# Feature units in pairs, three broadcasts later, the queries' low halves earlier

## The reference

```python
x = x + sliding_window_attention(rms_norm(x), positions, w_qkv, ..., w_o)
x = x + (silu(h @ w_gate) * (h @ w_up)) @ w_down
x = x + hybrid_mixer(rms_norm_2(x, g_mix), ...)
x = x + memory_cross_attention(rms_norm_2(x, g_cross), rms_norm_2(mem, g_mem), ...)
x = x + conv_glu_ffn(rms_norm_2(x, g_ffn), ...)
return rms_norm_2(x, g_final)
```

## Time and profile before

| | |
|---|---|
| median of three runs | 2711.31 us |
| the profiled execution, its own time | 2711.65 us |
| its span, first to last instruction | 2710.3 us |
| TensorE matmuls busy | 2698.5 us, 100% of the span |
| TensorE weight loads (beside the matmuls) | 2295.3 us, 85% |
| VectorE busy | 1690.4 us, 62% |
| ScalarE busy | 1370.2 us, 51% |
| mean granted clock of TensorE | 0.999 |
| DMA | 183 GB/s mean |

### The profile page before, as it was taken

How to read it: one execution, slowest core, us unless ns; L and a number is a source line. 1 busy time by engine, 2 the same in 40 slices (tenths; PEclk the granted TensorE clock), 3 DMA queues, 4 the chain that set the end, 5 groups by cost and what they waited for, 6 DMA issues and landing times.

```text
span 2710.3 us, 34758 instructions
## 1 busy us (share of the span) xinstructions
PE 2698.5 (100%) x13968; PEld 2295.3 (85%) x13968; DVE 1690.4 (62%) x2420; ACT 1370.2 (51%) x2036; POOL 0.2 (0%) x4
## 2 busy tenths in 40 slices
PE   9999999999999999999999999999999999999999
PEld 8778888888888888888888888888888888888887
DVE  7885666556656664664555655544568756785676
ACT  7875544344434454455444644444455535553554
POOL 0000000000000000000000000000000000000000
PEclk9999999999999999999999999999999999999999
DMA  7335566666665577768686555544556565656554
GB/s 245 125 110 178 186 188 190 194 185 188 194 193 185 189 198 169 172 144 193 185 196 220 174 184 189 189 145 156 185 176 210 182 206 178 197 181 205 186 187 155
DMA packets 257154, 495.64 MB, mean 183 GB/s; under 512 B 17313, under 2 KB 19105, under 8 KB 256482
## 3 DMA queue, kind: packets, MB, share of 16 engines
q1 hardware_dynamic: 256994, 493.43, 59.8%
HBM read 491.27 MB, written 2.10 MB: 182 GB/s over the span
## 4 chain that ended last, share of the span: by engine, by line
PE 98%; ACT 1%; DVE 1%; issue 0%; DMA 0%; SPq 0%; ACTq 0%
PE ps L500 29%; PE ps L489 16%; PE ps L490 16%; PE ps L491 16%; PE ps L505 15%; PE ps L457 2%; PE ps L697 1%; PE ps L613 1%; PE ps L758 1%; PE ps L739 1%; PE ps L590 0%; PE ps L663 0%; PE ps L586 0%; PE ps L650 0%; PE ps L711 0%
## 5 line engine op out<-in xcount | busy, mean ns | idle before, releaser
L954 ACT CAST whi<-raw 128x1024 fp32r<-128x1024 f32 x919 | 966.1, 1052 | 1224.9 <-PE ps L491 627.7
L1395 DVE TENSOR_TENSOR wlo<-raw,whi 128x1024 fp32r<-128x1024 f32 x919 | 1120.3, 1222 | 660.2 <-ACT whi L954 658.7
L500 PE MATMUL ps<-XA,whi 128*128 128x512 f32 x1792 | 449.1, 392 | 0.0
L500 PE MATMUL ps<-XC,whi 128*128 128x512 f32 x1664 | 416.9, 392 | 0.0
L489 PE MATMUL ps<-whi,XB 128*128 128x512 f32 x944 | 370.8, 393 | 2.2 <-issue 2.2
L500 PEld LDWEIGHTS ps<-XA,whi 128*128 128x128 f32 x1792 | 322.6, 189 | 57.9
L491 PE MATMUL ps<-whi,XB 128*128 128x512 f32 x944 | 368.3, 390 | 0.0
L490 PE MATMUL ps<-wlo,XB 128*128 128x512 f32 x944 | 368.2, 390 | 0.0
L500 PEld LDWEIGHTS ps<-XC,whi 128*128 128x128 f32 x1664 | 299.5, 189 | 53.7
L489 PE MATMUL ps<-whi,XA 128*128 128x512 f32 x736 | 292.1, 397 | 1.5 <-DVE wlo L1395 0.9
L491 PE MATMUL ps<-whi,XA 128*128 128x512 f32 x736 | 287.0, 390 | 0.0
(11 more groups left out here) (250 smaller groups left out, 1930.7 us busy)
## 6 DMA issues: line engine op xcount, KB each, us to landing
raw<-in_w_up SPq DMA_DIRECT2D x176, 512.0 KB, 3.6
raw<-in_w_in SPq DMA_DIRECT2D x128, 512.0 KB, 5.1
raw<-in_ffn_w_gate SPq DMA_DIRECT2D x88, 512.0 KB, 3.6
raw<-in_ffn_w_up SPq DMA_DIRECT2D x88, 512.0 KB, 4.1
raw<-in_ffn_w_down SPq DMA_DIRECT2D x88, 512.0 KB, 4.2
raw<-in_w_down SPq DMA_DIRECT2D x88, 512.0 KB, 3.7
raw<-in_w_ckv SPq DMA_DIRECT2D x64, 512.0 KB, 4.3
raw<-in_attn_w_qkv SPq DMA_DIRECT2D x39, 512.0 KB, 3.8
```

The costliest lines, as they stand in the source:

```text
L500: pe.matmul(ps[:, b, :], whi[:, i, j, c], both, start=w.begin and j == 0, stop=False)
L954: act.copy(whi[:, u % NSPL, :, :], raw[:, u % NRAW, :, :]).then_inc(s.hi, 1)
L1395: dve.tensor_tensor(wlo[:, u % NSPL, :, :], raw[:, u % NRAW, :, :], whi[:, u % NSPL, :, :].bitcast(F), ALU.subtract).then_inc(s.lo, 1)
```

## The change

`feature_unit` is cut into `feature_high` (the 8 matmuls with `whi`) and `feature_low` (the 8 with `wlo`). Where a feature unit has an even number, TensorE does its high part alone. At the next unit it does that unit's high part, then the low part of the first, then its own. The high part waits for `hi`, the low part for `lo`. What raises `unit` stays the last matmul of a unit's low part. Work that stands between the two units of a pair (transposes at units 73, 529 and 657) keeps its place ahead of the second unit.

Broadcasts 1, 4 and 5 move from two to four units behind their root, on TensorE and on ScalarE. In VectorE's program `queries_low` moves from the end of the query work to just behind the weight subtraction of its iteration, ahead of the residual sum, the feeds, the chances and `query_scale`.

```diff
--- before.py
+++ after.py
@@ -491,13 +491,18 @@
                     end = pe.matmul(o, xl, whi[:, i, j, :], start=False, stop=w.end and j == 1)
             end.then_inc(s.unit, 1)
 
-        def feature_unit(u, w):
+        def feature_high(u, w):
+
             i = u % NSPL
             for j in range(2):
                 both = X[w.x][:, w.xk + j, :, :]
                 for f in range(4):
                     b, c = w.banks[f], slice(f * P, (f + 1) * P)
                     pe.matmul(ps[:, b, :], whi[:, i, j, c], both, start=w.begin and j == 0, stop=False)
+
+        def feature_low(u, w):
+
+            i = u % NSPL
             for j in range(2):
                 high = X[w.x][:, w.xk + j, 0, :]
                 for f in range(4):
@@ -881,8 +886,10 @@
                     pe.wait_ge(s.ox, 8)
 
         q_turn, p_turn, p_values = later(Q, 4), later(ATTEND, 2), later(ATTEND, 3)
-        wide_at, level_at = later(ROOT, 2), later(LEVEL, 1)
+        wide_at, level_at = {u + (4 if n in (1, 4, 5) else 2): n for u, n in ROOT.items()}, later(LEVEL, 1)
         gla_turn_at, merge_at, c_turn_at = later(GLA, 3), later(MERGE, 25), later(CSC, 2)
+
+        PAIRS = {u for u in range(0, U_END, 2) if UNITS[u].kind == "feature"}
         pe.wait_ge(s.ones, 1)
         warm(8)
         for u, w in enumerate(UNITS):
@@ -929,11 +936,23 @@
                 banks_clear(u, w)
             if u > LAST - 4:
                 continue
-            pe.wait_ge(s.lo if u else s.lo0, u + 1)
             if w.kind == "rows":
+                pe.wait_ge(s.lo if u else s.lo0, u + 1)
                 rows_unit(u, w)
+            elif u - 1 in PAIRS:
+
+                pe.wait_ge(s.hi, u + 1)
+                feature_high(u, w)
+                pe.wait_ge(s.lo, u)
+                feature_low(u - 1, UNITS[u - 1])
+                pe.wait_ge(s.lo, u + 1)
+                feature_low(u, w)
             else:
-                feature_unit(u, w)
+                pe.wait_ge(s.hi, u + 1)
+                feature_high(u, w)
+                if u not in PAIRS:
+                    pe.wait_ge(s.lo, u + 1)
+                    feature_low(u, w)
 
         for u in range(LAST - 3, LAST + 1):
             pe.wait_ge(s.lo, u + 1)
@@ -1255,7 +1274,7 @@
 
         q_root_at, q_turn = later(Q, 2), later(Q, 4)
         p_turn, p_values = later(ATTEND, 2), later(ATTEND, 3)
-        wide_at, gla_root_at, gla_turn_at = later(ROOT, 2), later(GLA, 1), later(GLA, 3)
+        wide_at, gla_root_at, gla_turn_at = {u + (4 if n in (1, 4, 5) else 2): n for u, n in ROOT.items()}, later(GLA, 1), later(GLA, 3)
         merge_at, c_turn_at, level_exp_at = later(MERGE, 25), later(CSC, 2), later(LEVEL, 0)
         tiles1, tiles2 = later(TILES, 1), later(TILES, 2)
 
@@ -1904,6 +1923,8 @@
                 done += 1
             if u in (1, 3, 5):
                 feed(*FEED[u][0], (1,))
+            if u in q_scale:
+                queries_low(q_scale[u])
             if u in RESID and u < U_END:
                 residual(u, RESID[u])
             for n, c, bank in FEED.get(u, []):
@@ -1942,7 +1963,6 @@
                 keys_low()
             if u in q_scale:
                 query_scale(q_scale[u])
-                queries_low(q_scale[u])
             if u in TILES:
                 e, ch, which, f = TILES[u]
                 tile_sum(u, e, ch, which, f)
```

## The result

The changed kernel takes 2703.93 us, the median of 10 runs (2703.78 to 2704.76), against 2711.34 us for the kernel before (10 runs, 2710.18 to 2711.82). The ratio is 0.9974 with a 95% interval of 0.9966 to 0.9982: 7.4 us or 0.27% faster. The forecast was 2703.0. The profiled execution took 2703.85 us, its span is 2702.5 against 2710.3. The executions of the kernel before fall into two groups some 1.5 us apart, those of the changed kernel don't; what that does to the 7.4 us is taken up behind e8.

The account below looks back on a forecast made before the run. TensorE, busy over the whole span, was taken as the bound. The profiled 2711.65 - 4.6 (pairs) - 3.8 (queries' low halves) = 2703.2 us; as that execution lay 0.3 us over the median, 2703.0 was given, range 2700.8 to 2708.4.

Parts of the forecast that it names:

- edit 1: Feature units on TensorE run by twos, 16 highs then 16 lows: 0.022 us saved a pair, -4.6 us in all.
- Edit 3: Queries' low halves made earlier on VectorE, ending TensorE's "issue" wait in unit 45 and the low clock behind: -3.8 us.
- The first step: Unit 45: TensorE starts at 176.09 instead of 178.32, 2.23 us saved.
- The second: Nine matmuls behind unit 45's wait run at full clock, 2.12 instead of 3.70 us: 1.58 us saved.
- the surplus from the grouped rows: Feature units: a train of 8 highs behind lows takes 1.843 us against 1.814, a surplus of 0.029 us.
- Edit 2: Three broadcasts two units later, as pairs delay their identities: cost nothing; without the move about 0.7 us each.
- Buffers: Second feed-forward: the tightest subtraction's slack of 3.45 us shrinks by 1.8 us; 1.6 us left, cost nothing.
- the arrears' three late copies: Second feed-forward "up" chunks: three odd iterations might each add 1.8 us to VectorE's backlog, 5.5 us together.
- Rival C: Second feed-forward: VectorE's backlog makes TensorE wait 2.05 us in each of 11 "up" chunks, about 2726 us; chance 0.05.
- A: Feature units: the surplus grows with the lows, so pairing saves nothing; 2707.5 us, up to 2709; chance 0.23.
- B: Unit 45 is held by something else, or the clock falls anyway: 2706.7 down to 2704.5 us; chance 0.07.
- D: Feature units: no surplus at all after 16 lows, saving 10.8 and 3.8 us: 2696.7 us; chance 0.04.

Follow-up runs that it names:

- e8: Changed kernel with the queries' low halves moved between the chances and the query scale: 2705.51 us.
- e1: Kernel before with only the queries' low halves moved ahead of the chances, feature units singly: 2707.97 us.
- e2: Changed kernel with the queries' low halves back at their old place, pairs and later broadcasts kept: 2707.47 us.
- e7: e1 with low matmuls of 320 instead of 256 columns: 2800.08 us.
- e3: Changed kernel with all broadcasts two units behind their root again: 2706.21 us.
- e10: Changed kernel with feature units by fours and the old waits, casts held until the unit four back has ended: 2724.49 us.
- e5: Changed kernel with feature units by fours (32 highs, then 32 lows) and the other engines' waits freed: 2701.94 us.
- e4: e1 with each high matmul followed by the low of the same bank: 2721.26 us.

## Why the prediction was right

The way and the size were right: 2703.0 forecast, 2703.93 measured, inside the range. Of the 0.9 us between them 0.5 are edit 1's term and 0.3 the forecast's last step: it took off what the profiled execution of the kernel before lay over its median, and the changed kernel's profiled execution lies at its median (2703.85 and 2703.93).

**Edit 3, -3.8 us forecast.** In the traces it is 3.8 us at the end of unit 45, both steps as worked out: e1 goes on at 176.09 as expected, the changed kernel at 176.28, since its run lay 0.16 us later there, and the low clock is gone. The first step, 2.2 us, is paid back in every execution. The second, 1.6 us, was real but conditional: a stop of 1.6 us leaves the clock alone (e8), one of 2.2 us lowers it, by the times, in the upper group's executions alone. The prediction took it as certain from the one profile that it had. It is luck that 7 of the 10 runs beside the changed kernel were of the upper group: against the 2710.37 us beside e1 the same changed kernel is 6.4 us faster and not 7.4. The time of 2703.93 us isn't touched by this, because the changed kernel has no low clock at unit 45 in either case.

**Edit 1, -4.6 us forecast.** This term was 0.5 us too large. e2's span is 4.0 us under that of before, and the eight feature stretches of the changed kernel are together 4.1 us shorter. The step that was off is the surplus from the grouped rows. Its mean of 2.005 us a train holds a few trains with 0.08 us on their first step behind transposes and broadcasts, which a pair doesn't save. In trains without that the surplus is 0.027 and the net gain 0.020 us, and 213 x 0.020 = 4.3. The mechanism was as forecast: the surplus is bounded (16 and 32 lows), and lows 9 to 16 go at 0.120.

**The rule of the Trainium skill** ("TensorE: Matmul & The Clock Gate", "Wait — 56ns, not 53.3ns?") would have made edit 1 worth nothing; e2 shows 4.0 us. Its form, columns / 2.4 GHz and a fixed cost, fits even steps at three widths: 226.7, about 146 and 120 ns for 512, 320 and 256 columns (the middle one from 0.145 us in e7's timeline and from 120 + 92.1 us / 3456 = 146.7 ns in its time), with 13 ns instead of its 2.5.

**Edit 2, nothing forecast, about 0.7 us each without it.** e3: 1.7 us in the list of waits and 2.3 us in the time for three, as worked out from the chain behind unit 72 (the list counts idle time alone, the time also the longer steps around a stop).

**Buffers.** Forecast was a slack of 1.6 us at the tightest subtraction; it is 1.55. Of the arrears' three late copies only one counted. e10 shows what is behind that cover: at groups of four with the same waits it is used up, and TensorE waits. Rival C priced 11 chunks at 2.05 us; the late subtraction hits 8 at 1.85, because the last "up" chunk of each group of the second feed-forward is worked off in rows units.

**Rivals.** A is refuted by e5, B by e1 and e2, C by the missing waits (what it feared is seen in e10), D by the surplus that stays.

What stays open is what inside TensorE costs 0.027 us over five matmuls when the width rises, gives 0.007 back when it falls, and costs 0.004 us a turn when widths alternate (e4). The runs show that it is the width, not why. Open too is what decides in which executions the clock falls behind the stop of 2.2 us.

## What to carry to other kernels

When TensorE bounds a kernel, read start-to-start steps by their place in a train, not the mean of a group: in this kernel matmuls of one width in long trains are the cheapest order, and each return to a greater width costs about five slightly longer steps. Regrouping them delays the end of units, so count who gets buffers by those ends, and let each engine wait for the matmuls that read its own buffer. An "issue" wait that the profile can't name may be a semaphore with a late producer; where the clock falls behind it, a stop that is only somewhat shorter (1.6 instead of 2.2 us here) can already win the clock's part. And when the executions of one kernel fall into two groups, one profile shows only one of them: ask which cost the other doesn't pay before counting it as saved.

## What was not expected of the hardware

- The surplus behind a change of width: 0.027 us in all over the first five matmuls of 512 columns behind lows of 256, the same behind 8, 16 and 32 of them, and nearly the same behind 320 columns. It is zero behind 512.
- By turns, 512 and 256 columns take 0.353 us together, more than in trains of 8 (0.349), 16 (0.348) or 32 (0.347).
- Weight loads, one for each matmul, fit beside matmuls of 256 columns at 0.120 us a step with no gap that grows, over 32 in a row.
- The granted clock stayed at its higher level through a stop of 1.60 us and fell behind stops of 2.18 and 2.19 us at the same place, in the executions that were traced; in e2 it fell 1.1 us after TensorE had gone on. By the times, the stop of 2.2 us lowered it in only about half of the executions (31 of 62 of the kernel before, 8 of 11 of e2).
